# Merge stage of a hybrid encoder layer: three gate tiles first, y's statistics a group ahead, attention output through its own ring

## The chip, the cores and the metric

The kernel runs on one core of a Trainium2 chip. The metric is the device time of one execution in microseconds (us). The engines are TensorE (PE; PEld is its weight load), VectorE (DVE), ScalarE (ACT), GpSimd (POOL) and SyncE (SP), which here only issues DMA transfers. Each engine executes its own instructions in program order, and they wait for each other on semaphores.

## The reference

One layer of a streaming encoder for 512 prompt and 32 sample frames (with a gap of 4, TW = 548 columns). The part that matters here is the merge of the two token-mixer branches:

```python
y = y.reshape(b, T, D_INNER) * silu(z)                      # state-space branch, 2048 channels
yg = y.reshape(b, T, SSM_GROUPS, D_INNER // SSM_GROUPS)     # 8 groups of 256 channels
yg = yg * lax.rsqrt(jnp.mean(yg * yg, axis=-1, keepdims=True) + NORM_EPS)
y_ssm = yg.reshape(b, T, D_INNER) * p['ssm_norm']
...
g_ssm, g_att = jnp.split(sigmoid(gates), 2, axis=-1)
merged = g_ssm * (y_ssm @ p['w_ssm_out']) + g_att * (y_att @ p['w_att_out'])
x = x + g1 * rmsnorm(merged @ p['w_out'], p['norm_mix_post'])
```

## The kernel before

Everything lies transposed: channels on the 128 partitions, 548 frames as columns. Every large product is done in three passes to keep fp32 accuracy: weights and activations are split into a high part (ACT, a copy to fp32r) and a low part (the difference), and hi*hi, hi*lo and lo*hi are accumulated. A **tile** is one block of 1024x128 weights: 8 steps k, each of 3 passes times 2 column halves, so 48 matmuls of 128x274.

Weights come through one stream (`w`): SP loads tile n into one of 3 raw buffers (L139), ACT splits off the high part (`split_hi`, L155), POOL the low part (`split_lo`, L161), into one of 2 hi/lo buffers, and PE multiplies (L183). `split_hi(n)` waits until tile n-2 has been used up (`used` >= n-1).

The merge stage before the change runs, in the order of PE: one gate tile (the last of attention's gates, in PSUM slot 2); 8 tiles of `w_att_out` on the attention output (`hq_hi`, `hq_lo`), in slots 0 and 1 in turn; then 8 times a gate tile (slot 2) and two tiles of `w_ssm_out` on the normalized y (`wide_hi`, `wide_lo`). Beside the attention tiles the statistics of y are made, one group of 256 channels for each tile:

- SP loads y's group g into `yl[g % 4]` (`load_y`). From group 4 on it waits for `y_lo(g-4)`, the last reader of that buffer. The fourth of these buffers also holds attention output at the start (`al`), with `th` and `tmp[2]`.
- ACT squares the group (`square`, L1495); DVE adds its two halves (`add_squares`, L1548); PE sums over partitions with a matrix of ones (`sum_squares`, L1610), after the fifth k of an attention tile; ACT takes the root (`y_root`, L1501); DVE the reciprocal (L1569) and the two normalizing products (L1573).
- ACT makes the high part of the normalized y (`y_hi`, L1507), POOL the low part (`y_lo`, L1477). POOL's program has `y_lo(m-1)` behind `split_lo` of tile A0+m+2, and A0+m+2 is the stream's number of attention tile m+2. So that split waits until attention tile m has been used up.
- DVE multiplies each finished attention tile by its gate (`gated`, L1555), which frees the tile's PSUM slot: attention tile m waits for `gated(m-2)`.

Before the attention tiles, ACT and DVE split the 8 blocks of attention output (L1516, L1561), through 4 buffers. In the state-space part ACT turns each gate tile into a tanh (L1532), and DVE multiplies and adds (L1588, L1590). After the stage, `w_out` starts at L183 with `hp_hi` and `hp_lo` again.

Of the kernel before, what the change touches and what calls it, by code (L numbers as in the profile page):

```python
# [78 lines left out]
def build_layer(nc, i, o, scratch):  # L79
# [9 lines left out]
    with top:  # L89
# [1315 lines left out]
        with ExitStack() as st:  # L1405

            G1, A0 = 0, 1
            N1 = A0 + KB
            src = [i["w_gate"][8 + KB - 1]] + [i["w_att"][m] for m in range(KB)]
            for m in range(KB):  # L1410
                src += [i["w_gate"][m], i["w_ssm"][2 * m], i["w_ssm"][2 * m + 1]]
# [14 lines left out]
            with ExitStack() as ms:  # L1426
# [6 lines left out]
                al = [th[:], tmp[2][:], yl[Y_SLOTS - 1][:, 0, :], yl[Y_SLOTS - 1][:, 1, :]]  # L1433
                snorm = sb(ms, "snorm", [P, 16])
                (in_c, yn_s, yhi_s, ylo_s, th_s, m_s, dve_s, ahi_s, alo_s, ev_s, sq_s, add_s, ss_s, root_s, rec_s,
                 mhi_s, mlo_s) = sems(
                    ms, "m_c m_yn m_yhi m_ylo m_th m_m m_dve m_ahi m_alo m_ev m_sq m_add m_ss m_root m_rec m_mhi m_mlo")
# [3 lines left out]
                def sum_slot(g):  # L1441
                    return slot(3 - g % 2)

                with nc.Block(no_gpsimd_drain=True) as block:
                    @block.sync
                    def _(sp):
                        def load_y(g):
                            sp.dma_start(flat(yl[g % Y_SLOTS]), scratch["y"][g * P:(g + 1) * P, :]).then_inc(in_y[g % Y_SLOTS], 16)

                        load_y(0)  # L1450
                        for t in range(KB):
                            if t >= 4:
                                sp.wait_ge(alo_s, t - 3)
                            sp.dma_start(al[t % 4], scratch["att"][:, t, :]).then_inc(in_att[t % 4], 16)
                            if t == 3:
                                load_y(1)
                                sp.dma_start(snorm[:], i["ssm_norm"]).then_inc(in_c, 16)
                                w.load(sp, RAW_SLOTS)
                                load_y(2)
# [12 lines left out]
                    @block.gpsimd  # L1472
                    def _(pool):
                        def y_lo(g):
                            for t in range(2):
                                pool.wait_ge(yhi_s, 2 * g + t + 1)
                                pool.tensor_tensor(wide_lo[:, 2 * g + t, :], yl[g % Y_SLOTS][:, t, :],  # L1477
                                                   wide_hi[:, 2 * g + t, :].bitcast(F32), ALU.subtract).then_inc(ylo_s, 1)

                        for n in range(A0 + 2):  # L1480
                            w.split_lo(pool, n)
                        for m in range(GROUPS + 1):
                            w.split_lo(pool, A0 + m + 2)
                            if m >= 1:
                                y_lo(m - 1)
                        for n in range(A0 + GROUPS + 3, O0 + HL_SLOTS):
                            w.split_lo(pool, n)

                    @block.scalar
                    def _(act):  # L1490
# [6 lines left out]
                        def y_root(g):  # L1497
                            act.wait_ge(ss_s, g + 1)
                            if g >= 2:
# [8 lines left out]

                        w.split_hi(act, A0)
                        square(0)  # L1510
                        for t in range(KB):
                            if t == KB - 2:
                                act.wait_ge(w.used, G1 + 1)
                                act.activation(halves(mrg[:, KB - 1, :]), slot(2), ACT.Tanh, scale=0.5).then_inc(ev_s, 1)
                            act.wait_ge(in_att[t % 4], 16 * (t // 4 + 1))
                            act.activation(hq_hi[:, t, :], al[t % 4], ACT.Copy).then_inc(ahi_s, 1)  # L1516
# [10 lines left out]
                        for n in range(23):  # L1527
                            w.split_hi(act, N1 + n + 2)
                            if n % 3 == 0:
                                act.wait_ge(w.used, N1 + n + 1)  # L1530
                                act.wait_ge(m_s, KB + n // 3)
                                act.activation(halves(th[:]), slot(2), ACT.Tanh, scale=0.5).then_inc(th_s, 1)  # L1532
# [8 lines left out]
                    def _(dve):  # L1541
# [8 lines left out]
                        def gated(m):  # L1550
# [4 lines left out]
                            dve.scalar_tensor_tensor(out=halves(mrg[:, m, :]), in0=halves(mrg[:, m, :]), scalar=1.0, in1=slot(m % 2),  # L1555
                                                     op0=ALU.add, op1=ALU.mult).then_inc(m_s, 1)

                        add_squares(0)
                        for t in range(KB):
                            dve.wait_ge(ahi_s, t + 1)  # L1560
                            dve.tensor_tensor(hq_lo[:, t, :], al[t % 4], hq_hi[:, t, :].bitcast(F32), ALU.subtract).then_inc(alo_s, 1)  # L1561
                        dve.wait_ge(in_c, 16)
                        for m in range(KB):
                            if m >= 1:
                                gated(m - 1)
                            if m + 1 < GROUPS:
                                add_squares(m + 1)
                            dve.wait_ge(root_s, m + 1)
                            dve.reciprocal(rs[:, m % 2, :], rs[:, m % 2, :]).then_inc(rec_s, 1)  # L1569
                            dve.wait_ge(rec_s, m + 1)  # L1570
                            for t in range(2):
                                y = yl[m % Y_SLOTS][:, t, :]
                                dve.scalar_tensor_tensor(out=y, in0=y, scalar=snorm[:, 2 * m + t:2 * m + t + 1], in1=rs[:, m % 2, :],  # L1573
                                                         op0=ALU.mult, op1=ALU.mult).then_inc(yn_s, 1)
# [7 lines left out]
                        for m in range(KB):  # L1582
# [4 lines left out]
                            dve.wait_ge(w.used, N1 + 3 * m + 3)  # L1587
                            link(dve, dve.scalar_tensor_tensor(out=halves(tmp[0][:]), in0=halves(th[:]), scalar=1.0, in1=slot(m % 2),  # L1588
# [7 lines left out]
                    def _(pe):  # L1596
                        def tile(s, hi, lo, k0=0, nk=KB, sums=None):
                            for k in range(k0, k0 + KB):
                                w.multiply(pe, slot(s), hi[:, k, :], lo[:, k, :], k == 0, k == nk - 1)
                                if k == 6 and sums is not None:  # L1600
                                    sum_squares(sums)

                        def sum_squares(g):
                            pe.wait_ge(add_s, g + 1)
                            if g == 1:
                                pe.wait_ge(ev_s, 1)
                            elif g >= 2:
# [6 lines left out]
                        tile(2, hp_hi, hp_lo, sums=0)  # L1614
                        for m in range(KB):
                            if m >= 2:
                                pe.wait_ge(m_s, m - 1)
                            for k in range(KB):
                                if m == 0:
                                    pe.wait_ge(alo_s, k + 1)  # L1620
                                w.multiply(pe, slot(m % 2), hq_hi[:, k, :], hq_lo[:, k, :], k == 0, k == KB - 1)
                                if k == 4 and m + 1 < GROUPS:
                                    sum_squares(m + 1)
                        pe.wait_ge(root_s, GROUPS)
                        for m in range(KB):
                            if m >= 1:
                                pe.wait_ge(th_s, m)
                            tile(2, hp_hi, hp_lo)
                            if m == 0:
                                pe.wait_ge(ylo_s, 16)  # L1630
                                pe.wait_ge(m_s, KB - 1)
                            if m == 1:
# [3 lines left out]
                            tile(m % 2, wide_hi, wide_lo, 0, 16)  # L1636
                            tile(m % 2, wide_hi, wide_lo, 8, 16)
# [552 lines left out]
```

## Time and the profile before

| | us |
|---|---|
| median of 3 runs | 1434.98 (1433.67 to 1438.44) |
| the profiled execution | 1436.78 |
| its span, first to last instruction | 1435.0 |
| PE busy | 1339.5 (93%) |
| mean granted TensorE clock | 0.959 |

The profiled execution lies 1.8 us above the median, and 1.8 us of it lie outside its span. PE is busy nearly all the time in nearly every stretch. A time in the trace is counted from the span's start. The merge stage lies from 667.96 (its first matmul) to 912.98 (the last eighth of `w_out`'s first tile).

### The profile page before, as it was taken

Reading aid. Unit: us, or ns where it says so; the run is one execution under the profiler, and the core shown is the slowest. Engines: PE = TensorE matmul, PEld = TensorE weight load, DVE = VectorE, ACT = ScalarE, POOL = GpSimd, SP = SyncE. Lnnn points to the kernel's source line nnn. Section 1 sums busy time; section 2 is a strip of 40 time slices with the busy share of each in tenths; the row PEclk is TensorE's granted clock in tenths of the full one; section 3 lists DMA queues with packets and bytes.
Section 4 is the critical chain, followed back from the end, with each engine's and each line's share of the span. In section 5 each row is a group of like instructions: output and inputs, shape, how many; then the busy total and the mean of one; then the engine's idle time right before and its main releaser. Section 6 shows DMA issues by size and latency. Waiting matters only on the chain. (4 is left out here: it accounts for less than half of the span.)

```text
span 1435.0 us, 24802 instructions
## 1 busy us (share of the span) xinstructions
PE 1339.5 (93%) x10265; PEld 1255.5 (87%) x10265; DVE 809.9 (56%) x1288; ACT 508.1 (35%) x879; POOL 530.9 (37%) x315
## 2 busy tenths in 40 slices
PE   4699998999999999998798999988999999999996
PEld 1489988899899999998788999974899999999996
DVE  1745316898898898894780000337466666660105
ACT  2212425455455455453441222332332233332221
POOL 0533322332332333332464443332344444443443
PEclk8699989999999999999899999998799999999998
DMA  8275414433433433334331222541222222222221
GB/s 364 99 265 134 122 53 140 126 95 117 138 102 117 129 112 116 117 100 170 101 106 59 88 89 89 205 187 40 75 89 89 88 84 83 87 90 88 82 81 63
DMA packets 74015, 164.31 MB, mean 115 GB/s; under 512 B 28240, under 2 KB 42352, under 8 KB 70432
## 3 DMA queue, kind: packets, MB, share of 16 engines
q1 hardware_dynamic: 73904, 162.74, 35.2%
q8 instruction: 81, 1.33, 0.4%
q14 instruction: 30, 0.25, 0.1%
HBM read 147.10 MB, written 16.07 MB: 114 GB/s over the span
## 5 line engine op out<-in xcount | busy, mean ns | idle before, releaser
L161 POOL TENSOR_TENSOR w_lo<-raw_w,w_hi 128x1024 fp32r<-128x1024 f32 x174 | 429.0, 2466 | 730.3 <-ACT w_hi L155 730.3
L183 PE MATMUL psum<-hp_hi,w_hi 128*128 128x274 f32 x1472 | 449.8, 306 | 22.4 <-POOL hp_lo L284 13.4
L183 PE MATMUL psum<-hp_lo,w_hi 128*128 128x274 f32 x1472 | 430.9, 293 | 0.0
L183 PE MATMUL psum<-hp_hi,w_lo 128*128 128x274 f32 x1472 | 430.2, 292 | 0.0
L155 ACT ACTIVATE w_hi<-raw_w 128x1024 fp32r<-128x1024 f32 x174 | 184.1, 1058 | 547.0 <-PE psum L183 502.1
L183 PEld LDWEIGHTS psum<-hp_hi,w_hi 128*128 128x128 f32 x1472 | 281.7, 191 | 36.5 <-POOL hp_lo L284 16.1
L183 PEld LDWEIGHTS psum<-hp_lo,w_hi 128*128 128x128 f32 x1472 | 284.5, 193 | 1.3
L183 PEld LDWEIGHTS psum<-hp_hi,w_lo 128*128 128x128 f32 x1472 | 282.7, 192 | 0.0
L183 PE MATMUL psum<-hq_hi,w_hi 128*128 128x274 f32 x832 | 248.7, 299 | 12.5 <-POOL hq_lo L1677 8.5
L183 PE MATMUL psum<-hq_hi,w_lo 128*128 128x274 f32 x832 | 245.5, 295 | 0.0
L183 PE MATMUL psum<-hq_lo,w_hi 128*128 128x274 f32 x832 | 244.2, 294 | 0.0
L183 PEld LDWEIGHTS psum<-hq_hi,w_hi 128*128 128x128 f32 x832 | 161.3, 194 | 16.3 <-POOL hq_lo L1677 11.6
L183 PEld LDWEIGHTS psum<-hq_lo,w_hi 128*128 128x128 f32 x832 | 162.4, 195 | 0.4
L183 PEld LDWEIGHTS psum<-hq_hi,w_lo 128*128 128x128 f32 x832 | 160.8, 193 | 0.0
L1096 DVE SCALAR_TENSOR_TENSOR cv<-raw,gp_all,cv 128x548 f32<-128x548 f32 x96 | 93.1, 976 | 14.2 <-ACT cv L978 12.2
L183 PE MATMUL psum<-y_hi,w_hi 128*128 128x274 f32 x256 | 75.4, 295 | 6.2 <-POOL y_lo L1477 6.2
L1588 DVE SCALAR_TENSOR_TENSOR tmp<-th,psum 128x548 f32<-128x548 f32 x8 | 5.8, 723 | 126.2 <-PE psum L183 126.2
L183 PE MATMUL psum<-y_lo,w_hi 128*128 128x274 f32 x256 | 75.1, 293 | 0.0
L183 PE MATMUL psum<-y_hi,w_lo 128*128 128x274 f32 x256 | 75.0, 293 | 0.0
L1891 DVE COPY fr<-fpar 128x2 f32<-128x2 f32 x22 | 41.2, 1874 | 58.9 <-ACT fr L1866 58.9
L1902 DVE SCALAR_TENSOR_TENSOR fs<-th,tmp 128x548 f32<-128x548 f32 x22 | 53.0, 2408 | 32.1 <-ACT th L1873 32.1
L1123 DVE TENSOR_SCALAR dec<-acs_b,tok_all 128x128 f32<-128x128 f32 (+1 forms) x160 | 66.1, 473 | 8.4 <-PE psum L1272 8.4
(263 smaller groups left out, 2033.0 us busy)
## 6 DMA issues: line engine op xcount, KB each, us to landing
raw_w<-in_w_grp SPq DMA_DIRECT2D x58, 512.0 KB, 3.8
raw_w<-in_w_ffn_in SPq DMA_DIRECT2D x44, 512.0 KB, 3.6
ada<-in_w_ada SPq DMA_DIRECT2D x12, 1024.0 KB, 20.6
raw_w<-in_w_ffn_out SPq DMA_DIRECT2D x22, 512.0 KB, 3.5
acs_b<-mem_acs SPq DMA_DIRECT2D x8, 1096.0 KB, 5.6
raw_w<-in_w_ssm SPq DMA_DIRECT2D x16, 512.0 KB, 3.5
ada_o<-in_w_ada SPq DMA_DIRECT2D x4, 2048.0 KB, 11.3
raw_w<-in_w_qkv SPq DMA_DIRECT2D x13, 512.0 KB, 4.9
```

Of the source, the lines that this page charges most:

```text
L155: act.activation(flat(w_hi[self.hl_slot(n)]), raw_w[self.raw_slot(n)][:], ACT.Copy).then_inc(self.hi_done, 1)
L161: eng.tensor_tensor(flat(w_lo[self.hl_slot(n)]), raw_w[self.raw_slot(n)][:], flat(w_hi[self.hl_slot(n)]).bitcast(F32), ALU.subtract).then_ ...
L183: mm = pe.matmul(out[:, h, :], w, x[:, cols], start=first and j == 0, stop=last and j == 2)
L1096: ins = dve.scalar_tensor_tensor(out=cv[:, t, :], in0=raw[:, t, 1 + k:1 + k + TW], scalar=par(g, GP_W + 4 * t + k, GP_W + 4 * t + k + 1), ...
L1123: ins = dve.tensor_scalar(dec[u % 2][0:L, r, 0:L], acs_b[0:L, r, c0:c0 + L], tok_all[0:L, g, c, 2, r:r + 1], 0.0, ALU.add, ALU.min)
L1588: link(dve, dve.scalar_tensor_tensor(out=halves(tmp[0][:]), in0=halves(th[:]), scalar=1.0, in1=slot(m % 2), op0=ALU.add, op1=ALU.mult))
L1891: link(dve, dve.tensor_copy(r[:, LEAD + S0 - 2:LEAD + S0], fpar[:, f, 4:6]))
L1902: dve.scalar_tensor_tensor(out=sl[f % 2][:], in0=th[:], scalar=1.0, in1=c[:], op0=ALU.add, op1=ALU.mult).then_inc(fsl_s, 1)
```

## The change

- The stage now begins with three gate tiles (the last attention gate in slot 0, gate 0 in slot 1, gate 1 in slot 0 again). Gate 0 and 1 become tanh at once, in two buffers `ths`, instead of before their state-space tiles. The state-space part then runs two tiles, gate m+2, two tiles, and so on.
- `sum_squares(0)` stands in the second gate tile, `sum_squares(1)` in the third, and `sum_squares(m+2)` in attention tile m after the fourth k. Before, attention tile m held `sum_squares(m+1)`. ACT's `square` and `y_root` and DVE's `add_squares` stand correspondingly earlier in their programs; `y_hi`, `y_lo` and their order against the weight splits stay.
- On DVE the order is now reciprocal(g), `add_squares(g+2)`, `gated(g-2)`, normalize(g); it was `gated(m-1)`, `add_squares(m+1)`, reciprocal(m), normalize(m).
- The attention output has buffers of its own (`al0`, the two halves of `yl[3]`, `rs[:,1]`); blocks 4 and 5 have their low part made on POOL, the others on DVE. SP's order of loads is changed at the start.
- The first state-space tile waits for y's low parts step by step, not for all 16 at once. Attention tiles use slot (m+1)%2.
- The number of y buffers (`Y_SLOTS` = 4) is unchanged, and so is what `load_y(g)` waits for.

```diff
@@ SP
+                        load_y(0)
+                        load_att(0)
+                        load_y(1)
+                        load_att(1)
+                        load_att(2)
+                        load_att(3)
+                        sp.dma_start(snorm[:], i["ssm_norm"]).then_inc(in_c, 16)
+                        load_att(4)
+                        w.load(sp, RAW_SLOTS)
+                        load_y(2)
+                        load_att(5)
+                        load_att(6)
                         w.load(sp, RAW_SLOTS + 1)
-                        sp.wait_ge(alo_s, KB)
+                        load_att(7)
+                        w.load(sp, RAW_SLOTS + 2)
+                        wait_att_lo(sp, 5)
+                        wait_att_lo(sp, 6)
                         load_y(3)
-                        w.load(sp, RAW_SLOTS + 2)
                         w.load(sp, RAW_SLOTS + 3)
                         for g in range(Y_SLOTS, GROUPS):
                             w.load(sp, RAW_SLOTS + g)
                             sp.wait_ge(ylo_s, 2 * (g - Y_SLOTS + 1))
                             load_y(g)
@@ POOL
-                        for n in range(A0 + 2):
+                        for n in range(A0 + 1):
                             w.split_lo(pool, n)
+                        att_lo(4)
+                        att_lo(5)
+                        w.split_lo(pool, A0 + 1)
                         for m in range(GROUPS + 1):
                             w.split_lo(pool, A0 + m + 2)
                             if m >= 1:
                                 y_lo(m - 1)
@@ ACT
+                        w.split_hi(act, 1)
+                        square(0)
+                        att_hi(0)
+                        act.wait_ge(w.used, G1 + 1)
+                        act.activation(halves(mrg[:, KB - 1, :]), slot(0), ACT.Tanh, scale=0.5).then_inc(ev_s, 1)
+                        w.split_hi(act, 2)
+                        y_root(0)
+                        square(1)
+                        for t in range(1, 4):
+                            att_hi(t)
                         w.split_hi(act, A0)
...
+                        gate_tanh(0, 1, slot(1))
+                        att_hi(4)
+                        att_hi(5)
                         w.split_hi(act, A0 + 1)
-                        y_root(0)
+                        gate_tanh(1, 2, slot(0))
+                        att_hi(6)
+                        att_hi(7)
+                        y_root(1)
+                        square(2)
                         for m in range(GROUPS + 1):
-                            if m + 1 < GROUPS:
-                                square(m + 1)
-                                y_root(m + 1)
                             if m >= 1:
                                 y_hi(m - 1)
                             if m < GROUPS:
                                 w.split_hi(act, A0 + m + 2)
+                            if m + 2 < GROUPS:
+                                y_root(m + 2)
+                            if m + 3 < GROUPS:
+                                square(m + 3)
@@ DVE
+                        att_lo(6)
+                        att_lo(7)
+                        y_reciprocal(1)
+                        y_norm(1)
+                        add_squares(2)
+                        add_squares(3)
+                        for g in range(2, GROUPS):
+                            y_reciprocal(g)
+                            if g + 2 < GROUPS:
+                                add_squares(g + 2)
+                            gated(g - 2)
+                            y_norm(g)
+                        gated(KB - 2)
                         gated(KB - 1)
@@ PE
-                        tile(2, hp_hi, hp_lo, sums=0)
+                        tile(0, hp_hi, hp_lo)
+                        tile(1, hp_hi, hp_lo, 0, 2)
+                        pe.wait_ge(ev_s, 1)
+                        tile(0, hp_hi, hp_lo, 1, 4)
                         for m in range(KB):
-                            if m >= 2:
+                            if m < 2:
+                                pe.wait_ge(th_s, m + 1)
+                            else:
                                 pe.wait_ge(m_s, m - 1)
                             for k in range(KB):
                                 if m == 0:
-                                    pe.wait_ge(alo_s, k + 1)
-                                w.multiply(pe, slot(m % 2), hq_hi[:, k, :], hq_lo[:, k, :], k == 0, k == KB - 1)
-                                if k == 4 and m + 1 < GROUPS:
-                                    sum_squares(m + 1)
-                        pe.wait_ge(root_s, GROUPS)
+                                    wait_att_lo(pe, k)
+                                w.multiply(pe, att_slot(m), hq_hi[:, k, :], hq_lo[:, k, :], k == 0, k == KB - 1)
+                                if k == 3 and m + 2 < GROUPS:
+                                    sum_squares(m + 2)
```

ACT's program around the square of group 4 (`ysq<-yl0`, the first group that needs a y buffer again). Before, with the row that waits for attention tile 1 (`w_hi0<-raw_w0`) first:

```order
494 L155 ACTIVATE w_hi0<-raw_w0 128x1024 [waits m_used,m_landed0]
495 L1495 ACTIVATE ysq<-yl3 128x1096 [waits m_add,m_y3]
496 L1501 ACTIVATE y_rstd<-psum,consts 128x548 [waits m_yn,m_ss]
497 L1507 ACTIVATE y_hi<-yl1 128x548 [waits m_yn] x2
498 L155 ACTIVATE w_hi1<-raw_w1 128x1024 [waits m_used,m_landed1]
499 L1495 ACTIVATE ysq<-yl0 128x1096 [waits m_add,m_y0]
```

And of after, where the row that waits for attention tile 1 is `w_hi0<-raw_w2`:

```order
499 L1532 ACTIVATE ysq<-yl3 128x1096 [waits m_add,m_y3]
500 L1546 ACTIVATE y_hi<-yl0 128x548 [waits m_yn] x2
501 L155 ACTIVATE w_hi0<-raw_w2 128x1024 [waits m_used,m_landed2]
502 L1540 ACTIVATE y_rstd<-psum,consts 128x548 [waits m_yn,m_ss]
503 L1532 ACTIVATE ysq<-yl0 128x1096 [waits m_add,m_y0]
504 L1546 ACTIVATE y_hi<-yl1 128x548 [waits m_yn] x2
```

The square of group 4 stood behind the split that waits for attention tile 2; now it stands right behind the one that waits for tile 1.

DVE's program in the middle of the attention tiles (`tmp0<-ysq` is `add_squares` of an even group, `mrg<-mrg,psum` is `gated`, `yl<-yl,snorm,y_rstd` the normalizing). Before, group 2:

```order
762 L1555 SCALAR_TENSOR_TENSOR mrg<-mrg,psum 128x548 [waits m_used]
763 L1548 TENSOR_TENSOR tmp1<-ysq 128x548 [waits m_ss,m_sq]
764 L1569 RECIPROCAL y_rstd<-y_rstd 128x548 [waits m_root]
765 L1573 SCALAR_TENSOR_TENSOR yl2<-yl2,snorm,y_rstd 128x548 [waits m_rec]
766 L1573 SCALAR_TENSOR_TENSOR yl2<-yl2,snorm,y_rstd 128x548
```

After, from normalizing group 1 to group 2:

```order
757 L1629 SCALAR_TENSOR_TENSOR yl1<-yl1,snorm,y_rstd 128x548 [waits m_rec]
758 L1629 SCALAR_TENSOR_TENSOR yl1<-yl1,snorm,y_rstd 128x548
759 L1607 TENSOR_TENSOR tmp0<-ysq 128x548 [waits m_ss,m_sq]
760 L1607 TENSOR_TENSOR tmp1<-ysq 128x548 [waits m_ss,m_sq]
761 L1623 RECIPROCAL y_rstd<-y_rstd 128x548 [waits m_root]
762 L1607 TENSOR_TENSOR tmp0<-ysq 128x548 [waits m_ss,m_sq]
763 L1614 SCALAR_TENSOR_TENSOR mrg<-mrg,psum 128x548 [waits m_used]
764 L1629 SCALAR_TENSOR_TENSOR yl2<-yl2,snorm,y_rstd 128x548 [waits m_rec]
```

Row 762 is `add_squares(4)` and row 763 `gated(0)`, which frees attention tile 2's slot; before, `add_squares(3)` was the one in this loop turn, and it stood behind the `gated` of its turn.

## Rows read from the trace of the kernel before

**Rows 1.** The profile page, part 1: busy us, share of the span, instructions.
```profile
PE 1339.5 (93%) x10265; PEld 1255.5 (87%) x10265; DVE 809.9 (56%) x1288; ACT 508.1 (35%) x879; POOL 530.9 (37%) x315
```

**Rows 2.** Waits of PE, 667 to 766: us in total, times, longest.
```profile
PE psum L1610 <- DVE tmp L1548: 11.4, 7, 5.4
PE psum L183 <- POOL y_lo L1477: 6.2, 1, 6.2
PE psum L183 <- DVE hq_lo L1561: 3.0, 1, 3.0
```

**Rows 3.** Matmuls of PE in time: start, length, idle before.
```profile
701.54 0.29 PE L183 MATMUL psum<-hq_hi,w_lo 128*128 128x274 f32 x1
701.66 0.28 PE L183 MATMUL psum<-hq_hi,w_hi 128*128 128x274 f32 x1
...
706.22 1.19 PE L1610 MATMUL psum<-tmp,ones 128*128 128x274 f32 x4 [0.59 <-DVE tmp L1548]
707.05 0.49 PE L183 MATMUL psum<-hq_hi,w_hi 128*128 128x274 f32 x1
```

**Rows 4.** PE by stretches: length, busy (matmuls), granted clock, DMA share, GB/s.
```profile
686.00:693.00 7.00, 4.97 (x18) 0.50 0.37 124
740.00:747.00 7.00, 6.66 (x37) 0.76 0.15 58
764.00:771.00 7.00, 7.00 (x40) 0.66 0.01 3
771.00:778.00 7.00, 7.00 (x58) 1.00 0.13 35
```

**Rows 5.** ACT in order of time, 671 to 714.
```profile
671.61 1.12 ACT L1495 ACTIVATE ysq<-yl 128x1096 f32<-128x1096 f32 x1 [2.62 <-DMA yl<-mem_y]
...
683.05 1.05 ACT L155 ACTIVATE w_hi<-raw_w 128x1024 fp32r<-128x1024 f32 x1
684.12 1.28 ACT L1501 ACT_TABLE_LOAD   x1
685.41 0.72 ACT L1501 ACTIVATE y_rstd<-psum,consts 128x548 f32<-128x548 f32 x1
...
701.92 1.06 ACT L155 ACTIVATE w_hi<-raw_w 128x1024 fp32r<-128x1024 f32 x1 [0.52 <-PE psum L183]
...
712.41 1.12 ACT L1495 ACTIVATE ysq<-yl 128x1096 f32<-128x1096 f32 x1 [1.56 <-DMA yl<-mem_y]
```

**Rows 6.** POOL in order of time, 693 to 764.
```profile
705.53 3.20 POOL L1477 TENSOR_TENSOR y_lo<-yl,y_hi 128x548 fp32r<-128x548 f32 x2
...
752.67 2.39 POOL L161 TENSOR_TENSOR w_lo<-raw_w,w_hi 128x1024 fp32r<-128x1024 f32 x1 [0.56 <-ACT w_hi L155]
755.03 2.68 POOL L1477 TENSOR_TENSOR y_lo<-yl,y_hi 128x548 fp32r<-128x548 f32 x2
```

**Rows 7.** SP's DMA issues in time, and landing times of y and attention loads (tile yl).
```profile
667.93 0.33 SPq L1448 DMA_DIRECT2D yl<-mem_y  x1
...
708.75 0.33 SPq L1448 DMA_DIRECT2D yl<-mem_y  x1
...
DMA to landing us min/median/max: 3.4/5.0/7.6
```

**Rows 8.** DVE in order of time, 693 to 716.
```profile
701.82 1.49 DVE L1573 SCALAR_TENSOR_TENSOR yl<-yl,snorm,y_rstd 128x548 f32<-128x548 f32 x2
703.23 0.72 DVE L1555 SCALAR_TENSOR_TENSOR mrg<-mrg,psum 128x548 f32<-128x548 f32 x1
...
715.27 3.56 DVE L1569 RECIPROCAL y_rstd<-y_rstd 128x548 f32<-128x548 f32 x1
```

**Rows 9.** The low parts of attention output, and one sum of squares (tiles hq_lo, ysq): duration ns min/median/max.
```profile
L1677 POOL TENSOR_TENSOR hq_lo<-tmp,hq_hi x8: 1338/1640/1676, 993.1 to 1010.5; 128x548 fp32r<-128x548 f32 x8
L1561 DVE TENSOR_TENSOR hq_lo<-yl,hq_hi x4: 722/728/730, 675.3 to 683.3; 128x548 fp32r<-128x548 f32 x4
L1548 DVE TENSOR_TENSOR tmp<-ysq x8: 729/1258/2137, 672.8 to 739.6; 128x548 f32<-128x548 f32 x8
```

More of the change, by code:

```diff
@@ L1507, in y_hi @@
                                 act.activation(wide_hi[:, 2 * g + t, :], yl[g % Y_SLOTS][:, t, :], ACT.Copy).then_inc(yhi_s, 1)
-                        w.split_hi(act, A0)
[L1510 to L1516, printed above, removed]
@@ L1526, in _ @@
                                 w.split_hi(act, A0 + m + 2)
-                        for n in range(23):
+                            if m + 2 < GROUPS:
+                                y_root(m + 2)
+                            if m + 3 < GROUPS:
+                                square(m + 3)
+                        for n in range(21):
                             w.split_hi(act, N1 + n + 2)
[L1529 to L1532, printed above, removed]
+                            if n % 3 == 2 and n < 18:
+                                gate_tanh(n // 3 + 2, N1 + n, slot(2))
                         for t in range(KB):
@@ L1562, in _, with att_lo @@
-                        dve.wait_ge(in_c, 16)
[L1563 to L1574, printed above, removed]
+                        def att_lo(t):
+                            dve.wait_ge(ahi_s, t + 1)
+                            dve.tensor_tensor(hq_lo[:, t, :], al[t], hq_hi[:, t, :].bitcast(F32), ALU.subtract).then_inc(alo_s, 1)
@@ new lines, in y_reciprocal, with y_norm @@
+                        def y_reciprocal(g):
+                            dve.wait_ge(root_s, g + 1)
+                            dve.reciprocal(rs[:, g % 2, :], rs[:, g % 2, :]).then_inc(rec_s, 1)
+                        def y_norm(g):
+                            dve.wait_ge(rec_s, g + 1)
+                            for t in range(2):
+                                y = yl[g % Y_SLOTS][:, t, :]
+                                dve.scalar_tensor_tensor(out=y, in0=y, scalar=snorm[:, 2 * g + t:2 * g + t + 1], in1=rs[:, g % 2, :],
+                                                         op0=ALU.mult, op1=ALU.mult).then_inc(yn_s, 1)
@@ new lines, in _ @@
+                        add_squares(0)
+                        att_lo(0)
+                        y_reciprocal(0)
+                        add_squares(1)
+                        for t in range(1, 4):
+                            att_lo(t)
+                        dve.wait_ge(in_c, 16)
+                        y_norm(0)
+                        att_lo(6)
[3 more added lines that the diff above has]
+                        add_squares(2)
@@ L1596, in _, with tile @@
                     def _(pe):
[L1597 to L1600, printed above, removed]
+                        def tile(s, hi, lo, sums=None, at=None):
+                            for k in range(KB):
+                                w.multiply(pe, slot(s), hi[:, k, :], lo[:, k, :], k == 0, k == KB - 1)
+                                if k == at:
                                     sum_squares(sums)
@@ L1635, in _ @@
                                 pe.wait_ge(m_s, KB + m - 1)
-                            tile(m % 2, wide_hi, wide_lo, 0, 16)
-                            tile(m % 2, wide_hi, wide_lo, 8, 16)
+                            for k in range(16):
+                                if m == 0:
+                                    pe.wait_ge(ylo_s, k + 1)
+                                w.multiply(pe, slot(m % 2), wide_hi[:, k, :], wide_lo[:, k, :], k == 0, k == 15)
+                            if m + 2 < KB:
+                                if m == 0:
+                                    pe.wait_ge(root_s, GROUPS)
+                                else:
+                                    pe.wait_ge(th_s, m + 2)
+                                tile(2, hp_hi, hp_lo)
                         for k in range(KB):
```

77 lines of the change are left out of this document (45 added, 32 removed).

## The prediction, made before the changed kernel ran

> **What bounds the kernel now.** I read the busy times first: PE is busy 93% of the span, the next engine 56% [rows 1], so the kernel takes what PE works plus what PE waits, and an edit counts by the PE wait that it removes or makes. The list of PE's waits in the stretch of the edit comes next. It has 20.6 us: 11.4 for `add_squares` before the sums of squares, 6.2 for y's low part before the first state-space tile, 3.0 for the low part of the attention output [rows 2]. Those 20.6 us are all that this change can win there, apart from the clock. Then the matmuls themselves: 0.127 us from start to start, so a tile of 48 takes 6.1 us, and a sum of squares inside one makes it about 7.1 (0.83 to the next matmul, 0.2 more until the pace is back) [rows 3]. Last the granted clock: from 764 to 771, after the wait of 6.2, 40 matmuls start where 58 do in the next 7 us, and the clock column reads 0.66: 4.8 us at the lower level, 1.2 GHz, and 18 x 0.127 = 2.3 us lost, or 0.48 us for each us at that level. By that rate 686 to 693 lost 2.4 (4.97 busy at 0.50) and 740 to 747 lost 1.6, in all 6.3 us [rows 4].
>
> **What stays.** PE has the same 33 tiles and 8 sums. The tail of the stage and all behind it have the same order. The start at 667.96 is the same, since the first tile's weights are split ahead in both.
>
> **What goes.** The 3.0 us go: attention starts two tiles (13 us) later, with its data split. The 6.2 us mostly go too. The 11.4 us go in this form, since sums are asked for in other tiles. Removed: 20.6 us.
>
> **What comes first: the sum of group 2 in attention tile 0.** `sum_squares(2)` stands after the fourth k of attention tile 0. PE's work leads there at 667.96 + 6.1 + 7.1 + 7.1 + 3.1 = 691.4. When is `add_squares(2)` done? I add up the program orders. ACT: root(0), its table loaded early, ends at 678.1; square(1) (1.1) 679.2; three high parts 681.1; the split of tile 3 waits for tile 1's end, 681.2, and ends 682.5; table load and tanh (1.28 + 0.61) 684.4; the fourth block's high part 685.1. The next block is loaded only after DVE's second low part: DVE has reciprocal(0) (3.56) to 681.7, `add_squares(1)`, then that low part to 683.2 (0.73 each) [rows 8, 9]. A load that meets no queue lands 3.4 us later [rows 7], so high part 5 ends at 687.2. Tile 4's weights are issued behind block 6, at 686.2, among 1.6 MB in one bunch; I let them land at 690.5. Then split 1.06, tanh 0.6, two high parts 1.3, table load 1.28, root(1) 0.72: 695.5. DVE follows: reciprocal 3.57, normalize 1.5, add 0.73, with gaps of some 0.05 between them: 701.5. PE waits 701.5 - 691.4 = **10.1 us**. Bounds: if the weights are there when tile 2 has been used, the split starts at 688.6, and the wait is 8.2; if a load takes the 7.6 us of the slowest one [rows 7], it is 13.
>
> A table load costs 1.28 here, and the ACTIVATE behind it starts 0.01 us after it; nothing lies between it and the split before, either (683.05 + 1.05 = 684.10) [rows 5]. The Trainium skill (ScalarE: Activation LUTs, section What ACT_TABLE_LOAD costs) gives a switch of sets 2.66 us, 1.28 for the load and 1.38 for a drain. The change has two more switches, one of them on this chain, so the sum would be 1.4 us higher by the page; the rows show no room for such a drain, and I take the rows.
>
> **What comes next: the ring of four y buffers.** This is the large term. `square(4)` needs `load_y(4)`, which waits until POOL has made `y_lo(0)`, and that stands in POOL's program behind the weight split that waits for the end of attention tile 1 (E). That was so before, and the trace shows the chain: tile 1 ends at 701.66 (the last start plus 0.127) [rows 3], ACT splits at 701.92 [rows 5], POOL's `y_lo` ends at 708.73 [rows 6], SP issues the load at 708.75 [rows 7], the square starts at 712.41 [rows 5]. There the square was needed in attention tile 3. Now ACT has it right behind the split for E, and DVE has `add_squares(4)` ahead of `gated(0)`, without which attention tile 2 can't start. So tile 2 waits, and what it waits for begins with tile 1's end:
>
> 0.26 (to the split) + 1.14 (to POOL's start) + 2.39 + 2.68 (POOL, at the rows where DVE doesn't disturb it [rows 6]) + 0.02 + 3.66 (load) + 1.16 (square) + 0.75 (add) + 0.72 (`gated`) + 0.1 = **12.9 us**.
>
> Tiles 3, 4 and 5 wait in the same way for the ends of tiles 2, 3 and 4, through `load_y(5)` to `(7)`: each time the split for E, `y_lo`, the load, square, add, `gated`. Reciprocal and normalize (5.1) fit beside the running tile. Four waits: 4 x 12.9 = **51.6 us**. Nothing covers it: PE's queue is in order and its next matmul is the one that waits. Bounds of one: 12.2 with a load of 3.4 and the shortest steps, 14.5 if POOL takes 0.65 more as at 703 to 708.7 and the load, with a weight load issued just behind it, 5.0 (the median) [rows 7]. I take the load of 708.75, alone and after a pause as these are; the y load at 667.93 also landed in 3.68 with five transfers behind it [rows 5, 7].
>
> **Small ones.** Attention tile 1 waits for `add_squares(3)`, whose square is behind the split for tile 0's end: 0.26 + 1.06 + 0.72 + 1.12 + 0.8 = 4.0 against 3.05 of four k: 1.0. Attention tile 7 needs `gated(5)`, behind reciprocal(7), behind the root for the sum in tile 5: 0.4. The first state-space tile needs `gated(7)`, which can only start when tile 7 is done: 0.2 + 0.72 + 0.1 = 1.0. Its last two steps need `y_lo(7)`, on POOL behind another split: 1.1. Together 3.5.
>
> **The clock.** Five waits of 10 us and more, each followed by work. At 764, after 6.2 us, it cost 2.3; I take that for each, 11.5, against 6.3 before: +5.2. Below: 3 x 2.3 (that is, two of them free), +0.6. Above: the whole of what follows at 1.2 GHz, see the second rival.
>
> **Sum.** -20.6 + 10.1 + 51.6 + 3.5 + 5.2 = **+49.8 us**. The profiled execution of 1436.78 would become 1486.6; against the median of 1434.98 I forecast **1484.8 us**, 3.5% slower.
>
> **Rivals.**
> *The ring doesn't bind, and the change does what its order suggests* (faster). For this, `y_lo(0)` would have to be done well before tile 1 ends, or the square of group 4 be covered. Against it: POOL's order, which the change leaves alone, and the trace, where `y_lo` follows the split at once each time. Then the four waits drop out, the clock costs one stall: -20.6 + 10.1 + 3.5 - 6.3 + 2.3 = -11.0, and 1424.0. If DVE's add takes 2.1 instead of 0.73 beside POOL [rows 9], a group costs DVE 3.57 + 2.1 + 0.72 + 1.5 = 7.9 against PE's 7.1, 4 us in five groups, and it is 1428. It decides from the point where load plus `y_lo` end within 3 us of a tile's end.
> *The lower clock holds through each tile* (slower than forecast). A stalled period is 12.9 us idle and 7.1 us of work, more idle than any stretch of rows 4. At 0.48 us lost per us, work of 7.1 takes 13.7 at 1.2 GHz, 6.6 lost instead of 2.3, in four tiles, and 3.8 instead of 2.3 in the rest of tile 0: +18.7, 1503.5.
> *Only part of the ring's chain counts*: a y load or `y_lo` is ahead of its place for one or two groups, so that two of the four waits vanish: -2 x (12.9 + 2.3) = -30.4, 1454.4. I see no instruction order that would do it.
> *The head's wait is small* (the weights land at once, DVE earlier): at the bound of 8.2 it is only -1.9, inside the range.
>
> **How the numbers follow.** The forecast as worked out has 0.72; the held clock 0.12; half a ring 0.06; the ring that doesn't bind 0.09; a remainder of 0.01 for no change. The bounds of the forecast: low, four waits of 12.2 (-2.8), head 8.2 (-1.9), clock (-4.6): 1475.5; high, four waits of 14.5 (+6.4), head 13 (+2.9), some of the clock's surplus (+5): 1499. The range is 1474 to 1502, which leaves out half a ring, the free ring and the end of the held clock. What a measurement of this kernel can tell from no change is about 0.3%, 4.3 us. Faster by more: 0.09; within: 0.01; slower: 0.90.
>
> **What would show it.** Right: four waits of PE of 12 to 14 us before attention tiles 2, 3, 4 and 5, released by DVE's `gated`; before each, a square on ACT that waits for the DMA of y, issued as `y_lo` ends; one wait of about 10 us inside attention tile 0 before a sum of squares; the first state-space tile starting near 819 instead of 763.75; the clock lower after each wait. Wrong: if the y load is issued before the split that follows a tile's end, the ring term falls; if the waits are there but the sum in tile 0 comes without one, my head chain has an error of order; if the stretch is as long as I say but the end isn't later, PE's work behind it changed.

## The result, and the profile after

The changed kernel takes 1479.4 us (median of 4 runs, 1477.23 to 1482.55) against 1436.45 us before in the same set: a ratio of 1.0302, with a 95% interval of 1.0274 to 1.033. The forecast was 1484.8 us, with a range of 1474 to 1502. The changed kernel is slower by 43 us, as was forecast. The forecast of the time was 5 us too high; the forecast of the difference, 49.8 us, was 7 too high. The two differ by the 1.5 us that the kernel before took longer in this set than in the one that the prediction started from.

The page of the changed kernel, parts 1 and 2 (busy time, then PE in 40 slices and the granted clock in tenths):

```profile
PE 1340.5 (91%) x10265; PEld 1255.9 (85%) x10265; DVE 803.4 (54%) x1286; ACT 510.0 (34%) x881; POOL 530.7 (36%) x317
...
PE   4699989999999999997546999998799999999996
...
PEclk8699989999999999998868999998699999999998
```

PE's busy time is that of [rows 1] within 1 us, in a span of 1478.2 instead of 1435.0. In four slices in the middle (7, 5, 4 and 6 tenths) PE is busy little more than half of the time. The list of PE's waits, 667 to 830 (total, times, longest), answers [rows 2]:

```profile
PE psum L183 <- DVE mrg L1614: 50.8, 5, 12.5
PE psum L1686 <- DVE tmp L1607: 10.5, 2, 9.3
PE psum L183 <- POOL y_lo L1507: 0.7, 2, 0.4
```

That is 62.0 us instead of 20.6. The five waits for `gated` (L1614) are four of 12.4 to 12.5 before attention tiles 2 to 5, and one of 0.9 before the first state-space tile. The two waits for `add_squares` (L1607) are 9.3 in attention tile 0 and 1.2 in tile 1.

One of the four, before attention tile 2, engine by engine. PE's last matmul of tile 1 and first of tile 2, then ACT, POOL, SP and DVE (start, length, operation, idle before it):

```profile
713.09 0.29 PE L183 MATMUL psum<-hq_hi,w_lo 128*128 128x274 f32 x1
725.90 0.59 PE L183 MATMUL psum<-hq_hi,w_hi 128*128 128x274 f32 x1 [12.52 <-DVE mrg L1614]
```

```profile
713.47 1.06 ACT L155 ACTIVATE w_hi<-raw_w 128x1024 fp32r<-128x1024 f32 x1 [4.76 <-PE psum L183]
...
723.33 1.12 ACT L1532 ACTIVATE ysq<-yl 128x1096 f32<-128x1096 f32 x1 [8.19 <-DMA yl<-mem_y]
```

```profile
714.61 2.34 POOL L161 TENSOR_TENSOR w_lo<-raw_w,w_hi 128x1024 fp32r<-128x1024 f32 x1 [6.13 <-ACT w_hi L155]
716.91 2.63 POOL L1507 TENSOR_TENSOR y_lo<-yl,y_hi 128x548 fp32r<-128x548 f32 x2
```

```profile
719.56 0.33 SPq L1469 DMA_DIRECT2D yl<-mem_y  x1
```

```profile
724.48 0.73 DVE L1607 TENSOR_TENSOR tmp<-ysq 128x548 f32<-128x548 f32 x1 [11.93 <-ACT ysq L1532]
725.12 0.72 DVE L1614 SCALAR_TENSOR_TENSOR mrg<-mrg,psum 128x548 f32<-128x548 f32 x1
```

Read it from the bottom: `gated(0)` ends at 725.84 and PE starts at 725.90. In front of it stands an add that waits for a square; the square waits 8.2 us for the load of y's group 4; the load goes out at 719.56, as `y_lo(0)` ends (716.91 + 2.63 = 719.54); and `y_lo(0)` stands on POOL behind the split of weights whose high part waited for the end of attention tile 1. A tile's end is what starts the load that the next tile's start waits for.

### The profile page after: what moved, and what is told of

Its sections match the earlier page's. It is cut to its first block and busy times, and to the rows that moved or that the text cites. A ratio compares the mean times of both kernels' runs of the same rounds, so it can differ in the third digit from the quotient of the medians.

```text
span 1478.2 us, 24803 instructions
## 1 busy us (share of the span) xinstructions
PE 1340.5 (91%) x10265; PEld 1255.9 (85%) x10265; DVE 803.4 (54%) x1286; ACT 510.0 (34%) x881; POOL 530.7 (36%) x317
## 5 line engine op out<-in xcount | busy, mean ns | idle before, releaser
L183 PE MATMUL psum<-hp_hi,w_hi 128*128 128x274 f32 x1472 | 449.2, 305 | 23.3 <-POOL hp_lo L284 12.6
L183 PE MATMUL psum<-hq_hi,w_hi 128*128 128x274 f32 x832 | 251.6, 302 | 59.2 <-DVE mrg L1614 49.9
L941 POOL TENSOR_TENSOR xt<-xdt,tok_all 128x256 f32<-128x256 f32 (+1 forms) x40 | 24.5, 612 | 91.5 <-DVE xdt L1134 91.4
```

Of the source, the lines that this page charges most:

```text
L183: mm = pe.matmul(out[:, h, :], w, x[:, cols], start=first and j == 0, stop=last and j == 2)
L941: pool.tensor_tensor(xt[u % 2][0:L], xdt[u % 2][0:L], bcast_mid(tok_all[0:L, g, c, 1, :], HD), ALU.mult).then_inc(xt_s, 1)
```

## The experiments

Each edit is of the changed kernel unless it says otherwise; times are medians, beside runs of the kernel before (1433.7 to 1434.1 in these sets). The changed kernel itself was timed beside a kernel before of 1436.45, so a difference between its 1479.4 and a time below is 2 to 3 us smaller when both are taken against their own kernel before. The stage, from its first matmul to the last eighth of `w_out`'s first tile in the profiled execution, is given where it helps.

### The low part of y ahead of the weight split

```diff
 for m in range(GROUPS + 1):
-    w.split_lo(pool, A0 + m + 2)
     if m >= 1:
         y_lo(m - 1)
+    w.split_lo(pool, A0 + m + 2)
```

> Edit of the changed kernel: POOL makes y_lo(m-1) before the weight split of tile A0+m+2, not behind it. Theory (the ring of four y buffers): load_y(4) then goes out some 4 us after y_hi(0), at about 711.5 instead of 719.6, and lands before its square's turn. What is left of the chain from a tile's end is split 0.26+1.06, root 0.7, square 1.12, add 0.73, gated 0.72: four waits of 4.4 instead of 12.5, so -32 and some -4 of clock: 1479.4 becomes about 1443. Rival (it is only the order on DVE, gated behind add_squares, and the y load is beside the point): no change, 1479. Rival (DVE's throughput bounds the tiles, 7 to 8 us a group): about 1450 with waits of 1 to 2.

Measured: 1448.0 us, ratio to before 1.010 (1.0066 to 1.0133). PE's waits in the stage:

```profile
PE psum L183 <- DVE mrg L1614: 20.3, 5, 4.9
PE psum L1686 <- DVE tmp L1607: 10.6, 2, 9.3
```

The load of group 4 goes out at 710.14, and the four waits are 4.85 each. By exchanging two lines on POOL 31 us went by the medians, 29 when each is taken against its own kernel before, so the y load was in the chain, as the theory says. The time was expected at 1443; by itself it lies nearer to the 1450 of the rival in which DVE's throughput is the bound. The waits decide between the two: they are 4.85, where that rival has 1 to 2 and the theory 4.4. The add made them longer than my sum:

```profile
728.82 1.36 DVE L1607 TENSOR_TENSOR tmp<-ysq 128x548 f32<-128x548 f32 x1 [5.69 <-ACT ysq L1532]
```

Beside POOL's work it took 1.36 to 1.37 us before tiles 3 to 5 and 1.04 before tile 2, where the sum had 0.73; before tile 2 the square also waited 0.2 for the load. Of the 4 us of clock that I expected back little came: the stage is 32.3 us shorter, and 31.1 of that are PE's waits.

### A y buffer free much earlier

```diff
 # POOL; on ACT y_hi(m) takes the place of y_hi(m - 1) in the same way
-    w.split_lo(pool, A0 + m + 2)
-    if m >= 1:
-        y_lo(m - 1)
+    if m < GROUPS:
+        y_lo(m)
+    w.split_lo(pool, A0 + m + 2)
```

> Edit of the changed kernel: y_hi(m) and y_lo(m) stand one group earlier in ACT's and POOL's programs, before the weight split, so that a y buffer is free long before its next load is wanted. Theory: the y load drops out of the chain altogether, and what is left is the same as with y_lo ahead of the split: four waits of 4.4 us, about 1443; the time doesn't fall further although the loads go out still earlier. Rival (buffers and loads still limit in the other experiment): it falls below that one by more than 5 us.

Measured: 1446.8 us, ratio 1.0093 (1.0068 to 1.0117), not to be told from the experiment before. The loads go out earlier (group 4's at 698.10, which is 31.0 us after the stage's first matmul, where it was 45.3), and the waits for `gated` are the same to the tenth:

```profile
PE psum L183 <- DVE mrg L1614: 20.3, 5, 4.9
```

So with `y_lo` ahead of the split the ring of four no longer counts: what was wrong was where the instruction that frees a buffer stood. More than four buffers weren't tried. What is left, 4.85 a tile, is the chain split, root, square, add, gated.

### The gated product ahead of the add

```diff
 y_reciprocal(g)
+gated(g - 2)
 if g + 2 < GROUPS:
     add_squares(g + 2)
-gated(g - 2)
```

> Edit of the changed kernel: on DVE gated(g-2) stands before add_squares(g+2). Theory: the tile can start at once, but its sum of squares after the fourth k waits for the same y load: 12.5 - 0.7 - 3.05 = 8.7 us, four times, so -15: about 1464. The wait moves from the tile's first matmul (released by gated) to the sum (released by add_squares). Rival (the order on DVE is the cause): the four waits fall to about 1 us, some -46: 1433.

Measured: 1465.5 us, ratio 1.0217 (1.0197 to 1.0237). The wait has moved to the sums, and is shorter by the four k that now run ahead of it:

```profile
PE psum L1686 <- DVE tmp L1607: 46.2, 6, 10.0
...
PE psum L183 <- DVE mrg L1614: 0.9, 1, 0.9
```

The four waits before the sums of tiles 2 to 5 are 8.6, 8.8, 8.9 and 8.8 us, where 8.7 was expected; the rest of the 46.2 is the head's 10.0 and tile 1's 1.2. The gain is 14 us by the medians and 11 in the stage, which is 277.8. The rival, that DVE's order is the whole cause, had 1433 and falls.

### Both orders

> Edit of the changed kernel: y_lo(m-1) before the weight split on POOL, and gated(g-2) before add_squares(g+2) on DVE. Theory: what is left per tile is the wait of the sum of squares for the square behind the split, as in attention tile 1, where it is 1.2 us: -4 x 11.3 and the clock's -7: about 1427, clearly more than the sum of the two single edits (-36 and -15 would give 1428: the two add up only by accident, the waits tell: 1.2 us at the sum, none at the tile's start). Rival (DVE's throughput): it stops at about 1440, with DVE busy all the time.

Measured: 1434.8 us, ratio 1.001 (0.9992 to 1.0029), 8 us more than I expected. That leaves the time of the kernel before. PE's waits:

```profile
PE psum L1686 <- DVE tmp L1607: 12.5, 4, 9.2
PE psum L183 <- DVE mrg L1614: 7.8, 3, 3.5
```

Apart from the head's 9.2 the waits at the sums are 1.0 to 1.2, as expected. The surprise is two waits of 3.5 for `gated`, before tiles 3 and 5. DVE in order of time, ahead of one of them:

```profile
716.46 3.74 DVE L1629 SCALAR_TENSOR_TENSOR yl<-yl,snorm,y_rstd 128x548 f32<-128x548 f32 x2
720.12 3.56 DVE L1623 RECIPROCAL y_rstd<-y_rstd 128x548 f32<-128x548 f32 x1
723.61 0.66 DVE L1614 SCALAR_TENSOR_TENSOR mrg<-mrg,psum 128x548 f32<-128x548 f32 x1
```

The two normalizing products take 3.74 us together; in [rows 8] they took 1.49. Beside them POOL makes `y_lo` (715.99 to 719.62). With the other operations a group costs DVE 3.7 + 3.6 + 0.7 + 0.7 to 1.4 = 8.7 to 9.4 us. That is more than PE's 7.1, and near the rival of DVE's throughput, at a price that I had put on the add alone. It isn't the whole of that rival: DVE is not busy all the time, it stands idle 3.3 and 3.0 us before two of the adds, for the square. The time of 1434.8 lies between the theory's 1427 and the rival's 1440.

### The gated product ahead of the reciprocal too

This keeps `y_lo` ahead of the weight split, as in the experiment before it.

```diff
+gated(g - 2)
 y_reciprocal(g)
 if g + 2 < GROUPS:
     add_squares(g + 2)
-gated(g - 2)
```

> Edit of the kernel with both orders (y_lo first, gated before add_squares; 1434.8): gated(g-2) stands before reciprocal(g) too. There PE waits 12.5 us for the sums and 7.8 for gated, where I had expected only 1.2 a tile at the sums. Theory (order): the two waits of 3.5 for gated go, and some clock: about 1427. Rival (throughput of DVE beside POOL, 8.9 us a group): they come back as longer waits for the sums, 1432 to 1436.

Measured: 1431.4 us, ratio 0.998 (0.9962 to 0.9997). The waits for `gated` fall from 7.8 to 2.3, those for the sums rise from 12.5 to 15.1. Neither expectation is met (1427, and 1432 to 1436); the time lies a little below the rival's range. About half of what is taken from one wait comes back in the other, and the stage is 3.7 us shorter (239.2 against 242.9).

### The sum of group 2 at the head

```diff
 # ACT
 att_hi(5)
+square(2)
 w.split_hi(act, A0 + 1)
 ...
 y_root(1)
-square(2)
 # DVE
 y_norm(0)
+add_squares(2)
 att_lo(6)
 ...
-add_squares(2)
 add_squares(3)
```

> Edit of the changed kernel: square(2) on ACT before the split of tile 4's weights, add_squares(2) on DVE right behind normalizing group 0. Theory: the wait of 9.3 us before the sum of group 2 in attention tile 0 falls to 0 to 1; tile 1's wait for group 3 grows by 1, since its y load can't go out earlier: -8 and -1.6 of clock: about 1470. Rival (the wait is the weights' or the attention data's, not the square's): it turns into a wait of the same tile for hq_lo or w_lo, no gain, 1479.

Measured: 1469.3 us, ratio 1.0256 (1.0221 to 1.0291), 10 us below the changed kernel, or 7 when each is taken against its own kernel before; the stage is 282.2, also 7 shorter. PE's waits of the head:

```profile
PE psum L1686 <- DVE tmp L1607: 2.6, 1, 2.6
...
PE psum L183 <- DVE hq_lo L1619: 1.0, 1, 1.0
```

The 9.3 of tile 0 become 1.0, for the low part of the attention output, and tile 1's 1.2 become 2.6. PE's waits are 6.7 us less in all, so the 1.6 of clock that I expected back didn't show. So the head's wait was the place of `square(2)` and `add_squares(2)` in two programs, behind loads that they don't need.

### Keeping PE busy in the four waits

```diff
 # before attention tiles 2 to 5, ahead of the wait for gated
+pe.wait_ge(root_s, m + 1)
+for n in range(80):
+    pe.matmul(sum_slot(m)[:, n % 2, :], hq_hi[:, 0, 0:P], hq_hi[:, 1, 0:HW], start=True, stop=True)
 pe.wait_ge(m_s, m - 1)
```

> Edit of the changed kernel: in the four waits before attention tiles 2 to 5, PE computes 80 matmuls of 128x274 on data that is there, into a PSUM bank that nobody reads, 80 x 0.127 = 10.2 us, so inside the waits of 12.5. They add work and change no result. Theory: the waits stay as long from tile end to tile start, and only the lower clock after them goes: about 1.4 to 2.6 us a tile, together -7 to -8: about 1472. Rival (the lower clock costs as I forecast, 2.3 us for each): -9 or more: 1470. Rival (the clock is most of the loss): -20: 1460. If the fill delays the tiles, it gets slower.

Measured: 1476.6 us, ratio 1.030 (1.0267 to 1.0333): by the medians 2.8 less than without, but the ratios to the kernel before are the same (1.030 and 1.0302), so the runs show no gain. The profiled executions, one of each kernel, do. PE from 710 to 800 (length, busy, granted clock, DMA share, GB/s), in the changed kernel and then with the filling:

```profile
710.00:800.00 90.00, 40.11 (x237) 0.72 0.16 55
```

```profile
710.00:800.00 90.00, 80.10 (x587) 0.96 0.17 61
```

The clock is up, and the stage is 285.3 instead of 289.0 us, 3.7 less, half of what I expected. The tiles show why it is half. Tiles 3 and 5 ran at nearly full pace, 7.1 us; tiles 2 and 4 still took 8.7 and 8.6, although PE stood idle only 2.3 to 2.6 us between the filling and each of the four. In the first 7 us of tile 2 (723 to 730) the granted clock was 0.76, against 0.73 without the filling. So the filling is no full test of what the clock costs: in two of the four tiles the clock fell all the same.

### One part alone in the kernel before: y's low parts step by step

```diff
-pe.wait_ge(ylo_s, 16)
...
-tile(m % 2, wide_hi, wide_lo, 0, 16)
-tile(m % 2, wide_hi, wide_lo, 8, 16)
+for k in range(16):
+    if m == 0:
+        pe.wait_ge(ylo_s, k + 1)
+    w.multiply(pe, slot(m % 2), wide_hi[:, k, :], wide_lo[:, k, :], k == 0, k == 15)
```

> Edit of the kernel before, one part of the change alone: the first state-space tile waits for y's low parts step by step, not for all 16 at once. Theory: the wait of 6.2 us at 757.5 goes, since the last low part is there at 763.7 and is wanted at about 768: -6.2 and -2.3 of clock: 1436.5 becomes 1428. Rival (another wait takes its place, as for gated or for weights): within 3 us of before.

Measured: 1426.0 us, ratio 0.9953 (0.9936 to 0.9971): 7.7 us faster than the kernel before, where 8.5 was expected. The wait of 6.2 is gone from the list, and none stands in its place. This part of the change is good by itself.

### All of it early

```diff
 # ACT; POOL has y_lo(m) before the split, DVE gated before add_squares; head as above
 for m in range(GROUPS + 1):
-    if m >= 1:
-        y_hi(m - 1)
-    if m < GROUPS:
-        w.split_hi(act, A0 + m + 2)
+    if m < GROUPS:
+        y_hi(m)
     if m + 2 < GROUPS:
         y_root(m + 2)
     if m + 3 < GROUPS:
         square(m + 3)
+    if m < GROUPS:
+        w.split_hi(act, A0 + m + 2)
```

> Edit of the changed kernel, with all that the waits point to: y_hi and y_lo a group earlier and before the weight split, on ACT root and square before the split too, gated before add_squares on DVE, square(2) and add_squares(2) early at the head. Theory: no wait of a y load, of the sums or of gated is left but 1 to 2 us in tile 1, 0.9 before the first state-space tile and some tenths: PE's waits in the stage fall from 62 to about 4 us, and the clock stays up: 1436.5 (the kernel before) - 16.6 - 6.3 = about 1414, faster than both. Rival (DVE is the next bound: reciprocal 3.57, add, gated and normalize are 6.5 to 7.9 us a group against 7.1 of PE): about 1420. Rival (a weight split late on ACT): waits for w_lo, above 1425.

Measured: 1414.6 us, ratio 0.9878 (0.985 to 0.9906): faster than both kernels. PE's waits from 680 to 790 are 9.0 us, not 4:

```profile
PE psum L183 <- DVE mrg L1614: 6.4, 6, 1.8
PE psum L1686 <- DVE tmp L1607: 1.6, 1, 1.6
PE psum L183 <- DVE hq_lo L1619: 1.0, 1, 1.0
```

That the time is the expected 1414 is partly luck. The sum took 22.9 off 1436.5; in this set the kernel before ran at 1433.7, and the gain is 19.1. The 5 us of waits more than expected, most of them for `gated` before tiles 2 to 6, cover what is missing. They point to the rival in which DVE is the next bound, though it expected 1420.

The last experiment puts `gated(g-2)` ahead of the reciprocal here too:

> Edit of the kernel with all early (1414.6): on DVE gated(g-2) stands before reciprocal(g), not behind it. There PE still waits 6.4 us before tiles for gated. Theory (an order on DVE: 3.6 us of reciprocal stand in the way of a gated whose tile is long done): 5.5 of the 6.4 go, to about 1409; the 0.9 before the first state-space tile stays. Rival (DVE's throughput: its normalizing takes 3.6 instead of 1.5 beside POOL's y_lo, 8.2 us of DVE a group against 7.1 of PE): the waits move to the sums of squares or come back at the tiles, and the time stays within 2 us of 1414.6.

Measured: 1414.3 us, ratio 0.9869 (0.9846 to 0.9892). The runs show no gain, as the rival of DVE's throughput says, and the theory's 1409 is not reached. The waits for `gated` are down to 0.9, and those for the sums are up from 1.6 to 4.3:

```profile
PE psum L1686 <- DVE tmp L1607: 4.3, 3, 1.6
PE psum L183 <- DVE mrg L1614: 0.9, 1, 0.9
```

With 0.5 for the attention output, PE's waits are 5.7 instead of 9.0, and in the profiled execution the stage is 4.1 us shorter (222.4 against 226.5). A gain of that size lies at the edge of what the two intervals can tell, so whether this order is worth something small stays open. All engines from 700 to 750 in this last kernel (PE, PEld, DVE, ACT, POOL busy us, clock, DMA share, GB/s):

```profile
700.00:750.00 50.00, 46.30 (x343) 44.81 (x343) 48.08 (x30) 22.78 (x29) 36.98 (x22) 1.00 0.35 113
```

DVE is busy 48.1 of 50 us, so it is the next bound in these tiles. Of the 5.5 us that this exchange took from the waits for `gated`, 2.7 came back at the sums; other orders weren't tried.

## Why the prediction was right, step by step

**The ring of four y buffers.** Forecast 12.9 us, four times, before tiles 2 to 5; measured 12.52, 12.37, 12.48 and 12.52, together 49.9 against 51.6. (The list counts a wait from the modelled end of the last matmul. Counted as in the forecast, from 0.127 after its start, the first is 12.68, so that 0.2 of it is error and the rest the way of counting.) The chain's rows stand above: split at 0.25 after tile 1's end, POOL at 1.4, the load out at 6.3, the square at 10.1, `gated` done at 12.6. Each point of the chain is within 0.2 of where the sum had it; the add and the product overlap by a tenth. It is shown, not only argued: with `y_lo` ahead of the split the waits fall to 4.85, and freeing the buffers still earlier changes nothing more. The rival in which the ring doesn't bind needed another order on POOL; that order was the first experiment, and it gave 1448 and not 1424, since I had forgotten there that the rest of the chain, split, root, square, add, gated, has no cover either. That rival's price was wrong: without the y load the change still has four waits of 4.85. The rival with half a ring falls, as all four waits came. The upper bound of one wait was summed wrongly: 12.9 + 0.65 for POOL + 1.34 for a load of 5.0 is 14.9, not 14.5, which would have put the upper bound of the time at 1501, still inside the stated range.

**The head.** Forecast 10.1 us, measured 9.3. The weights of tile 4 were there at 688.39, that is 22.15 after the stage's first matmul, and I had put 690.5 - 667.96 = 22.5. The chain ran in the order written, and the rest of the 0.8 is steps that overlap by about a tenth each.

**The small ones.** Tile 1: forecast 1.0, measured 1.2. Tile 7: 0.4, not seen. The first state-space tile: 1.0, measured 0.9. Its last steps: 1.1, measured 0.7. That tile was to start near 819 and started at 813.08: 1.7 of the difference is the stage's earlier start, 2.8 the shorter waits, and the rest the clock.

**What goes.** All of the 20.6 us of [rows 2] went in their old form, as assumed. That much of it could be won is shown by the step-by-step wait in the kernel before (7.7 us for the 6.2 and its clock) and by the kernel with all of it early, which has 9.0 us of waits left.

**The clock.** This term was mis-sized. I gave each of five waits 2.3 us, 11.5 in all. In the profile after, tiles 2 to 5 take 8.9, 8.5, 9.7 and 8.9 us from start to end instead of 7.1, which is 7.6 us, and the end of tile 0 takes 5.8 instead of 4.1: 9.3 us in all. The granted clock after the first of the four waits (length, busy, granted clock, DMA share, GB/s):

```profile
726.00:733.00 7.00, 7.00 (x39) 0.73 0.00 0
```

0.73 against 0.66 after the wait of 6.2 in [rows 4], so 3.8 us at 1.2 GHz instead of 4.8: a wait twice as long on the average cost less clock (1.9 a tile; the four are 1.8, 1.4, 2.6 and 1.8). The second rival, in which the lower clock holds through each tile, falls. Filling the waits with matmuls gave back 3.7 of the 7.6 us. The clock column there has 0.96 over 90 us, which is 7.2 us at 1.2 GHz, and at 0.48 lost for each us that accounts for 3.5 more; tiles 2 and 4, at 8.7 and 8.6, are where it was lost.

**The sum.** From the stage's first matmul to the last eighth of `w_out`'s first tile it was 245.0 us before (667.96 to 912.98) and is 289.0 after (666.24 to 955.23): +44.0. PE's waits make 62.0 - 20.6 = 41.4 of it, and 2.6 are left for the clock, where I had 5.2. (The count of the tiles above gives 9.3 after and the prediction 6.3 before, so 3.0, which agrees within half a us.) Against the forecast of 49.8 that is 1.7 less in the ring, 0.8 in the head, 0.7 in the small ones and 2.6 in the clock. The changed kernel's stage began 1.7 us earlier; the wait of PE at the stage's start varied between 1.2 and 2.7 us over the runs here, for nothing in the edits.

**The table loads.** The change has two more, as expected. ACT at the one that stands on the head's chain:

```profile
691.08 1.28 ACT L1540 ACT_TABLE_LOAD   x1
692.37 0.72 ACT L1540 ACTIVATE y_rstd<-psum,consts 128x548 f32<-128x548 f32 x1
```

The high part before it ran from 690.41 for 0.65 us, so it ended at 691.06. The switch costs 1.3 us. The Trainium skill (ScalarE: Activation LUTs, section What ACT_TABLE_LOAD costs) gives 2.66 with its drain; in these rows there is no drain, and the measurement decides.

## What to carry to other kernels

If work is moved a stage ahead, follow not only what it computes but what frees its buffers: the load of a ring's next entry is issued by the last reader of the old one, and if that reader stands in its engine's queue behind something that waits for the current tile, each tile's end starts a fresh DMA latency. Then put the freeing instruction ahead of the waiting one; here two exchanged lines on POOL were worth 29 to 31 us, and freeing the buffers still earlier was worth nothing beyond that. And an instruction that frees an accumulator (`gated`) shouldn't stand behind one that waits for a load (11 to 14 us here).

## What the runs showed of the hardware

DVE operations with two inputs in SBUF become slow beside POOL's. The two normalizing products took 1.49 us [rows 8] or 1.48 alone. Beside `y_lo` or a weight split they took 3.6 to 3.74 in most groups of the kernels with both orders and with all early, and 3.07 in the first experiment. The reciprocal, with one input, took 3.56 to 3.58 throughout, and `gated`, with one input in SBUF and one in PSUM, 0.66 to 0.73. One such stretch in the kernel with all early, DVE and then POOL:

```profile
719.93 3.62 DVE L1629 SCALAR_TENSOR_TENSOR yl<-yl,snorm,y_rstd 128x548 f32<-128x548 f32 x2
723.48 3.56 DVE L1623 RECIPROCAL y_rstd<-y_rstd 128x548 f32<-128x548 f32 x1
```

```profile
720.02 2.95 POOL L161 TENSOR_TENSOR w_lo<-raw_w,w_hi 128x1024 fp32r<-128x1024 f32 x1 [1.93 <-ACT w_hi L155]
```

In the same kernel, at 713.83, where POOL stands idle from 713.32 to 715.37, the two products took 1.48. The products above end at 723.55, 0.6 us after POOL's split (722.97), which is a little less than one product takes: the second seems to have waited until the split was nearly done. The Trainium skill (GPSIMD Engine Reference, section Key points) says that POOL shares its SBUF interfaces with VectorE, with contention for DVE instructions with two SBUF inputs; the trace agrees, and adds the price, some 2 us a time for this pair. With it a group costs DVE about 8 us in the fastest kernels here, against PE's 7.1 a tile; at the durations alone (3.56 + 0.73 + 0.72 + 1.49) it would be 6.5. That removing the contention would lift the bound wasn't tried: an edit that moves `y_lo` off POOL would show it.
